# A reordered front of the expert layer in a two-layer diffusion backbone on one Trainium2 core

## The chip, the core and the metric

One NeuronCore of a Trainium2 chip runs the whole program. Its engines each have their own instruction stream: PE (TensorE, matrix products into the eight banks of PSUM), DVE (VectorE), ACT (ScalarE), POOL (GpSimd, which here issues the gathers) and SP (SyncE, which issues plain loads). Streams are ordered among each other by semaphores alone. The metric is the device time of the program in microseconds (us).

## What is computed

The reference is one inference step of a trunk of two layers over 640 tokens (128 context, 512 latent) of width 1024, in float32. Layer 0 mixes tokens by windowed attention beside a Mamba-2 scan, layer 1 by a bidirectional gated recurrence. Each layer then applies an output projection and a mixer of single-neuron experts (PEER), and this is the part that matters here:

```python
        out, new = even_mixer(h, P, j, ctx)        # or odd_mixer; ends in  mix @ w_out
        x = x + g1 * out
        h = rms_norm(x, P['norm_ffn'][l]) * (1 + sc2) + sh2
        x = x + g2 * peer(h, P, l)
...
def peer(h, P, l):
    q = (x @ P['p_w_q'][l]).reshape(m, PEER_HEADS, 2, PEER_DKEY)
    s = jnp.einsum('mhpd,hpnd->mhpn', q, P['p_sub_keys'][l])
    top_s, top_i = lax.top_k(s, PEER_TOPK)
    cand_s = top_s[:, :, 0, :, None] + top_s[:, :, 1, None, :]
    best_s, best_pos = lax.top_k(cand_s, PEER_TOPK)
    act = jax.nn.gelu(jnp.einsum('pd,phkd->phk', xb, u[eb])) * softmax(best_s)
    out = jnp.einsum('phk,phkd->pd', act, v[eb])
```

Every token picks 16 experts for each of 8 heads, so 128 rows of 4 KB from the table u and 128 from the table v.

## The kernel before

The tokens lie as 5 tiles of 128. `project_and_peer` runs once per layer. Its **front** is: the output projection of the five tiles, the update of x, the normalised input of the experts for tile 0, the router scores of tile 0, and the first top-k. Its **loop** is 40 steps g (tile t = g // 8, head i = g % 8); each step gathers 16 rows of u and 16 of v for every token (a gather is 512 KB and is one POOL instruction), takes 16 dot products with u on DVE, and adds 16 weighted rows of v on PE.

Nothing schedules this code: each engine runs its list in the order in which it is written, and waits where a `wait_ge` stands. The lists are:

- **PE.** In layer 0 first 40 transposes of the mixed rows (`rows(t, c)`, 8 per tile, L561, into banks 0 and 1, so each tile waits until ACT has copied the one before out at L494); layer 1 has these already. Then `project(t, b)`: tile t times half b of the output weights, 8 products into bank 6 + b (L533), with `score(0, n)` (a quarter of the router scores of tile 0, L553) and `turn(0)` (8 transposes of the normalised tile, L541) between them. `project(t, b)` for t >= 1 waits until DVE has read the same bank for tile t - 1 (`so.ev`). After all of them come the expert sums (L596).
- **DVE.** `projected(t)`: for both halves multiply the bank by the gate (L364) and add to x (L367). `normed(t)` (L373, L374). `topk(g)`: from L383 (first maximum) to L409 (the 16 expert numbers). `head(g)`: 16 dots (L429) and a tail of small operations to the weights at L445. The order is projected 0, normed 0, projected 1, topk 0, projected 2, topk 1, copy of the tile to PSUM (`h2p`, L457), topk 2, head 0 (with projected 3 after its eighth dot), topk 3, projected 4, head 1, and then topk(g + 2), head(g).
- **ACT.** Copies of transposes and scores out of PSUM (L494, L483, L488), the statistics of x (L476 to L478), and in the loop the diagonal weight matrices (L521).
- **POOL.** For each slot in turn the gather of u for step g (L344) and that of v for step g - 1 (L352), each into a ring of 8 buffers: a gather of u waits for the dot that reads its buffer (`s.ufree`), one of v for the sums that read it (`s.vfree`). Alone the first gather of v waits besides for all ten projections (`so.mm` at 10, a wait that ends at L533), since its ring lies over the output weights.
- **SP.** In layer 0 half 0 of the output weights (`load_out`, L1213), then in both layers the router weights of 6 MB and 2 MB (L298, L299), and behind them two modulation rows spread over all partitions (`bcp`, L301), which `normed(0)` reads. Half 1 of the output weights is loaded earlier, in `attention`.

Of the kernel before, what the change touches and what calls it, by code (L numbers as in the profile page):

```python
# [295 lines left out]
def router_weights(m, sp, l):  # L296

    sp.dma_start(m.wqA[:, :, :], m.wqk_rows[l][:, 0:12, :]).then_inc(m.sems.pw.h, 16)  # L298
    sp.dma_start(m.wqB[:, :, :], m.wqk_rows[l][:, 12:16, :]).then_inc(m.sems.pw.h, 16)  # L299
    for k in range(2):  # L300
        sp.dma_start(m.bcp[:, k, :], m.mod[l * 12 + 3 + k:l * 12 + 4 + k, :].to_broadcast([P, D])).then_inc(m.sems.pbc.h, 16)  # L301


def project_and_peer(nc, m, l, out):
# [8 lines left out]

    with nc.Block() as block:
        @block.sync
        def _(sp):
            if rows:
                load_out(m, sp, m.w_out, 0)
# [36 lines left out]
        def _(dve):  # L355
            ch = Link(dve, s.cv)

            def projected(t):
                for b in range(2):
# [4 lines left out]
                    nc.vector.tensor_tensor(m.oproj[:, :], ps[6 + b][:, :], m.gate[:, cond_of(t), b * 512:(b + 1) * 512], ALU.mult).then_inc(so.ev.h, 1)  # L364
# [54 lines left out]
            def head(g):  # L419
# [32 lines left out]
            projected(2)  # L452
            topk(1)
            for g in range(STEPS):
# [16 lines left out]
        def _(act):  # L471
# [8 lines left out]
            def turned(t):  # L480
                act.wait_ge(s.ptp.h, s.ptp.at(t + 1))
                for b in range(2):
                    q = nc.scalar.activation(m.phT[:, 4 * b:4 * b + 4, :], ps[(2 if t == 0 else 6) + b][:, :].rearrange("p (c t) -> p c t", c=4), ACT.Copy)  # L483
                q.then_inc(s.pht.h, 1)

            def scored(t, n):
                act.wait_ge(s.pqp.h, s.pqp.at(4 * t + n + 1))
                nc.scalar.activation(m.S[:, t % 2, n * 512:(n + 1) * 512], ps[n if t == 0 else 6 + n % 2][:, :], ACT.Copy).then_inc(s.pse.h, 1)  # L488

            if rows:  # L490
                for t in range(TILES):
                    act.wait_ge(so.tp.h, so.tp.at(t + 1))
                    for b in range(2):
                        q = nc.scalar.activation(m.mixT[:, t, 4 * b:4 * b + 4, :], ps[b][:, :].rearrange("p (c t) -> p c t", c=4), ACT.Copy)  # L494
                    q.then_inc(so.tpe.h, 1)
            statistics(0)
            turned(0)
            scored(0, 0)
            scored(0, 1)
# [1329 lines left out]
```

## Time and profile before

| | us |
|---|---|
| median of three runs | 4979.14 |
| lowest, highest of them | 4977.14, 4986.17 |
| the profiled execution, its own time | 4986.78 |
| span of the profiled execution, first to last instruction | 4984.9 |
| front of layer 0, from the first transpose to the first gather of v | 679.76 to 795.11 |
| front of layer 1, from the first projection to the first gather of v | 3195.12 to 3303.70 |

The profile gives for one execution each engine's busy time, what it waited for, and a timeline. The loops fill most of the span. PE is busy for 3952.8 us (79%), DVE for 3105.3 us (62%), POOL for 2672.2 us (54%), and 1508.39 MB pass through the 16 DMA engines, 1347.37 MB of them as gathers. A wait is put down to what ended it; an engine's idle time counts only where something later waits for that engine.

### The profile page before, as it was taken

The page shows a single profiled execution, that of the slowest core. Times are in us where ns is not written, and L with a number is a line of the kernel's source. Part 1 is how long each engine was busy: PE and PEld are TensorE (multiplying, and loading weights), DVE is VectorE, ACT ScalarE, POOL GpSimd, SP SyncE. Part 2 cuts the span into 40 slices and gives each one's busy share as a digit, 9 for nine tenths or more (in the row PEclk, how much of TensorE's full clock was granted, in tenths as well). Part 3 has the DMA queues.
Part 4 walks back from the last instruction along what each step waited for, and adds up shares of the span by engine and source line. Part 5 has one row for each costly group of instructions (what it writes and reads, how often), then busy time and mean ns, then how long its engine had stood idle before and what let it go on. Part 6 is the DMA issues. An engine that isn't in the chain of part 4 may idle for free. (4 is left out here: it accounts for less than half of the span.)

```text
span 4984.9 us, 41356 instructions
## 1 busy us (share of the span) xinstructions
PE 3952.8 (79%) x11732; PEld 1830.7 (37%) x11732; DVE 3105.3 (62%) x8304; ACT 1054.0 (21%) x2804; POOL 2672.2 (54%) x2872
## 2 busy tenths in 40 slices
PE   6596698887877877877788888587878879779777
PEld 2354563332322322322256665432323323223222
DVE  0124747777777677676425656377677777777774
ACT  1202231111111111111235454101111111111111
POOL 1100005777777777777532322047777777777775
PEclk8896799999999999999999999799999999999999
DMA  9910028999999999999911011169999999999998
GB/s 391 370 48 10 24 97 309 397 402 405 395 404 404 389 409 405 386 404 409 335 50 47 24 47 36 77 259 409 390 409 394 401 402 392 409 408 392 409 408 347
DMA packets 456205, 1508.39 MB, mean 303 GB/s; under 512 B 50838, under 2 KB 99894, under 8 KB 455228
## 3 DMA queue, kind: packets, MB, share of 16 engines
q0 software_dynamic: 371104, 1347.37, 68.5%
q1 hardware_dynamic: 80284, 141.82, 7.9%
q10 hardware_dynamic: 4608, 16.78, 0.8%
q8 instruction: 86, 1.41, 0.1%
q14 instruction: 123, 1.01, 0.1%
HBM read 1484.84 MB, written 20.94 MB: 302 GB/s over the span
## 5 line engine op out<-in xcount | busy, mean ns | idle before, releaser
L596 PE MATMUL psall<-work 128*128 128x512 f32 x5120 | 2445.6, 609 | 650.3 <-DMA work<-in_p_v,idx 586.5
L429 DVE CUSTOM_DVE_ANT_0 work<-work,psall 128x1024 f32<-128x1024 f32 x1280 | 1519.3, 1219 | 870.3 <-DMA work<-in_p_u,idx 869.7
L344 POOL DMA_INDIRECT work<-in_p_u,idx x1280 | 1214.5, 949 | 977.1 <-DVE idx L409 479.5
L596 PEld LDWEIGHTS psall<-work 128*128 128x128 f32 x5120 | 891.8, 190 | 2199.1 <-issue 1118.5
L352 POOL DMA_INDIRECT work<-in_p_v,idx x1280 | 1216.1, 950 | 498.2 <-issue 332.2
L521 ACT ACTIVATE work<-ident,work 128x128 f32<-128x128 f32 x1280 | 487.4, 399 | 1935.0 <-PE psall L596 1896.6
L1375 PE MATMUL psall<-work 128*128 128x512 f32 x640 | 284.1, 597 | 9.0 <-ACT work L1467 5.3
L553 PE MATMUL psall<-work 128*128 128x512 f32 x640 | 278.3, 592 | 0.0
L1348 POOL TENSOR_SCALAR work<-work 128x256 f32<-128x256 f32 x40 | 33.8, 844 | 381.2 <-ACT work L1459 381.2
L1570 DVE TENSOR_TENSOR work<-psall,work 128x128 f32<-128x128 f32 x560 | 116.7, 285 | 99.1 <-ACT work L1486 99.1
L553 PEld LDWEIGHTS psall<-work 128*128 128x128 f32 x640 | 121.6, 190 | 153.1 <-issue 153.1
L1375 PEld LDWEIGHTS psall<-work 128*128 128x128 f32 x640 | 119.5, 192 | 145.6 <-issue 145.6
L533 PE MATMUL psall<-work 128*128 128x512 f32 x320 | 150.5, 631 | 24.1 <-DVE work L364 21.7
L511 ACT ACTIVATE work<-work 128x16 f32<-128x16 f32 x80 | 17.3, 216 | 658.3 <-DVE work L435 658.3
L220 DVE TENSOR_TENSOR work<-psall,work 2x512 f32<-2x512 f32 x24 | 16.4, 684 | 197.3 <-PE psall L173 197.1
L157 POOL DMA_DIRECT2D mod_rows<-work x24 | 12.0, 506 | 199.4 <-DVE work L220 101.3
L173 PE MATMUL psall<-work 128*2 128x512 f32 x384 | 78.2, 691 | 48.0 <-DMA work<-in_w_ada 47.8
L1538 DVE TENSOR_TENSOR work<-psall,ident 128x128 f32<-128x128 f32 x40 | 11.7, 292 | 153.9 <-PE psall L1428 153.9
L429 DVE DVE_READ_ACCUMULATOR2_ANT work<- 128x1 f32 x1280 | 105.3, 82 | 0.0
L533 PEld LDWEIGHTS psall<-work 128*128 128x128 f32 x320 | 64.6, 204 | 107.2 <-issue 82.2
L1543 DVE COPY_PREDICATED work<-lmask,psall 128x128 f32<-128x128 uint8 x280 | 84.5, 302 | 29.6 <-DVE work L1543 1.4
L774 PE MATMUL psall<-work 128*128 128x512 f32 (+2 forms) x320 | 99.0, 470 | 0.0
(274 smaller groups left out, 3684.5 us busy)
## 6 DMA issues: line engine op xcount, KB each, us to landing
work<-in_w_ada SPq DMA_DIRECT2D x64, 768.0 KB, 12.3
work<-in_p_u,idx POOLq DMA_INDIRECT x1280, 8.2
work<-in_p_v,idx POOLq DMA_INDIRECT x1280, 8.3
work<-in_o_w_in SPq DMA_DIRECT2D x40, 512.0 KB, 7.0
work<-in_p_w_qT SPq DMA_DIRECT2D x32, 512.0 KB, 13.8
wqk_rows<-work ACTq DMA_DIRECT2D x32, 512.0 KB, 7.3
work<-wqk_rows SPq DMA_DIRECT2D x2, 6144.0 KB, 20.7
work<-mod_rows SPq DMA_DIRECT2D x16, 512.0 KB, 9.3
```

What stands on the lines that cost most here:

```text
L173: q = nc.tensor.matmul(m.ps[3 * (g % 2) + j][32 * j:32 * j + 2, :], m.condT[:, k, :], m.wa[:, n % WRING, j * 512:(j + 1) * 512], start=(k ...
L344: nc.gpsimd.indirect_dma_start(m.ur[:, b, :], None, u_flat, bass.IndirectOffsetOnAxis(ap=e, axis=0)).then_inc(s.ud[b].h, 16)
L352: nc.gpsimd.indirect_dma_start(m.vr[:, b, :], None, v_flat, bass.IndirectOffsetOnAxis(ap=e, axis=0)).then_inc(s.vd[b].h, 16)
L429: nc.vector.tensor_tensor_reduce(m.ur[:, b, :], m.ur[:, b, :], m.h2p[:, :], 1.0, 0.0, ALU.mult, ALU.add, m.d16[:, j:j + 1]).then_inc(s.ufr ...
L521: nc.scalar.activation(m.dgb[:, j % DIAGS, :], m.ident[:, :], ACT.Copy, scale=m.wt[:, t % 2, i * TOPK + j:i * TOPK + j + 1]).then_inc(s.dg ...
L533: q = nc.tensor.matmul(ps[6 + b][:, :], m.mixT[:, t, k, :], m.ew[:, b, k, :], start=(k == 0), stop=(k == KC - 1))
L553: q = nc.tensor.matmul(ps[n if t == 0 else 6 + n % 2][:, :], m.phT[:, k, :], w[:, :, k * P:(k + 1) * P], start=(k == 0), stop=(k == KC - 1))
L596: q = nc.tensor.matmul(o[:, k * 512:(k + 1) * 512], m.dgb[:, j % DIAGS, :], m.vr[:, b, k * 512:(k + 1) * 512], start=(i == 0 and j == 0), ...
L774: q = nc.tensor.matmul(m.ps[n % 8][:, 0:width], m.hT[:, k, c * P:(c + 1) * P], m.ew[:, p % 2, k, 0:width], start=(k == 0), stop=(k == KC - 1))
L1375: nc.tensor.matmul(ps[0][:, :], m.hT[:, k, t * P:(t + 1) * P], m.ow[:, b, k, 0:4, :].rearrange("p g n -> p (g n)"), start=(k == 0), stop=( ...
L1543: q = nc.vector.copy_predicated(m.So[:, t, :], m.lmask[:, l, :], ps[5 + r // 4][:, (r % 4) * P:(r % 4 + 1) * P])
L1570: q = nc.vector.tensor_tensor(out_v, in_v, ref, ALU.subtract)
```

## The change

It edits the front alone, in both layers, and one pair of buffers of attention.

1. The projections alternate between two pairs of banks: even tiles in 6 and 7, odd tiles in 0 and 1 (`bank(t)`). `project(t, b)` now waits for the read of tile t - 2.
2. The transposes of the mixed rows in layer 0 alternate between banks 4, 5 and 2, 3 and are spread over the front: tiles 0 and 1, two projections, tiles 2 and 3, and tile 4 behind `score(0, 0)`. `turn(0)` uses banks 4 and 5, the scores of tile 0 banks 2 and 3. ACT's copies follow (`mixed(t)`).
3. PE takes the projections of tile 3 ahead of `score(0, 1)`.
4. DVE runs topk 0, topk 1, then the copy to `h2p` (behind the copies out of those banks), projected 2 and head 0. Topk 2 and projected 4 come after head 0, and topk 3 stands after the eighth dot of head 1.
5. SP loads the `bcp` rows ahead of the router weights. Half 0 of the output weights of layer 0 is loaded in `attention`, whose buffers `pr` and `pT` move out of its place.
6. Two new waits: POOL's first gather of u in layer 0 waits for the last transposes of the mixed rows, and PE's first expert sum waits until DVE has read tile 3's projection (before: until ACT had copied two score banks).

```diff
 def router_weights(m, sp, l):
+    for k in range(2):
+        sp.dma_start(m.bcp[:, k, :], ...).then_inc(m.sems.pbc.h, 16)
     sp.dma_start(m.wqA[:, :, :], m.wqk_rows[l][:, 0:12, :]).then_inc(m.sems.pw.h, 16)
     sp.dma_start(m.wqB[:, :, :], m.wqk_rows[l][:, 12:16, :]).then_inc(m.sems.pw.h, 16)
-    for k in range(2):
-        sp.dma_start(m.bcp[:, k, :], ...).then_inc(m.sems.pbc.h, 16)
...
+    def bank(t):
+        return 6 if t % 2 == 0 else 0
...
-            if rows:
-                load_out(m, sp, m.w_out, 0)
...
                             pool.wait_ge(s.ix.h, s.ix.at(g + 1))
+                            if g == 0 and rows:
+                                pool.wait_ge(so.tp.h, so.tp.at(TILES))
...
                     if g == 0 and j == RING:
                         projected(3)
+                    if g == 1 and j == RING:
+                        topk(3)
...
             topk(0)
-            projected(2)
             topk(1)
+            dve.wait_ge(s.pht.h, s.pht.at(1))
+            if rows:
+                dve.wait_ge(so.tpe.h, so.tpe.at(TILES))
...
-                if g + 2 < STEPS:
+                if g == 0:
+                    projected(2)
+                elif g == 1:
+                    topk(2)
+                    projected(4)
+                elif g + 2 < STEPS:
                     topk(g + 2)
-                if g == 1:
-                    projected(4)
                 head(g)
...
             def project(t, b):
                 if t == 0:
                     pe.wait_ge(sw[b].h, sw[b].at(16))
-                else:
-                    pe.wait_ge(so.ev.h, so.ev.at(2 * t + b - 1))
+                if t >= 2:
+                    pe.wait_ge(so.ev.h, so.ev.at(2 * t + b - 3))
+                if rows and b == 0:
+                    pe.wait_ge(so.tpe.h, so.tpe.at(t + 1))
...
+            mix(0)
+            mix(1)
             project(0, 0)
             project(0, 1)
+            mix(2)
+            mix(3)
             project(1, 0)
             turn(0)
             project(1, 1)
             score(0, 0)
+            mix(4)
             project(2, 0)
             project(2, 1)
+            project(3, 0)
+            project(3, 1)
             score(0, 1)
-            for t in (3, 4):
-                project(t, 0)
-                project(t, 1)
+            project(4, 0)
+            project(4, 1)
             score(0, 2)
             score(0, 3)
...
-    q = Arena(st)
+    q = Arena(15360)
     m.pr = q.take(3, 512)
     m.pT = q.take(2, 512)
...
+            load_out(m, sp, m.e_w_out[0], 0)
             load_out(m, sp, m.e_w_out[0], 1)
```

PE's list in the front of layer 0, before. L561 are the transposes of the mixed rows, L533 projections (8 products each), L541 the turned tile, L553 scores, L596 expert sums:

```order
298 L561 MATMUL psall<-ident,work 128x128 x40
299 L533 MATMUL psall<-work 128x512 x24
300 L541 MATMUL psall<-ident,work 128x128 x8
301 L533 MATMUL psall<-work 128x512 x8
302 L553 MATMUL psall<-work 128x512 x8
303 L533 MATMUL psall<-work 128x512 x16
304 L553 MATMUL psall<-work 128x512 x8
305 L533 MATMUL psall<-work 128x512 x32
306 L553 MATMUL psall<-work 128x512 x16
307 L596 MATMUL psall<-work 128x512 x96
```

The same place now, where the lines are L584, L550, L560, L574 and L627 in that order:

```order
298 L584 MATMUL psall<-ident,work 128x128 x16
299 L550 MATMUL psall<-work 128x512 x16
300 L584 MATMUL psall<-ident,work 128x128 x16
301 L550 MATMUL psall<-work 128x512 x8
302 L560 MATMUL psall<-ident,work 128x128 x8
303 L550 MATMUL psall<-work 128x512 x8
304 L574 MATMUL psall<-work 128x512 x8
305 L584 MATMUL psall<-ident,work 128x128 x8
306 L550 MATMUL psall<-work 128x512 x32
307 L574 MATMUL psall<-work 128x512 x8
308 L550 MATMUL psall<-work 128x512 x16
309 L574 MATMUL psall<-work 128x512 x16
```

Sixteen transposes instead of 40 now stand ahead of the first projection, and four projections instead of two stand between the first and the second score; the counts are the same.

DVE's list around the second top-k of layer 0, before (L409 ends the second top-k, L457 is the copy to `h2p`, L383 begins the third top-k):

```order
393 L409 TENSOR_SCALAR idx<-work 128x16
394 L457 COPY psall<-work 128x1024
395 L383 MAX work<-work 128x8
396 L384 MAX_INDEX ti<-work 128x8
397 L385 MATCH_REPLACE work<-work 128x128
```

The same place now (L413 ends the second top-k, L465 is the copy, L368 and L371 are projected(2), L435 the first dot of head 0):

```order
389 L413 TENSOR_SCALAR idx<-work 128x16
390 L465 COPY psall<-work 128x1024
391 L368 TENSOR_TENSOR work<-psall,gate 128x512
392 L371 TENSOR_TENSOR x<-x,work 128x512
393 L368 TENSOR_TENSOR work<-psall,gate 128x512
394 L371 TENSOR_TENSOR x<-x,work 128x512
395 L427 TENSOR_TENSOR work<-work 128x16
396 L435 ISA work<-work,psall 128x1024
```

The third top-k has left the place between the copy and the first dot, and projected(2) has come from ahead of the second top-k to it.

## Rows read from the trace of the kernel before

**Rows 1.** the page's chain that ended last, share of the span by engine
```profile
DMA 9%; POOL 9%; DVE 8%; PE 5%; issue 4%; ACT 0%; SPq 0%; DVEq 0%; POOLq 0%
```

**Rows 2.** stretches: us; busy (count) of PE, PEld, DVE, ACT, POOL; clock; DMA; GB/s
```profile
679.70:695.40 15.70, 9.81 (x40) 7.84 (x40) 0.00 (x0) 5.42 (x10) 0.00 (x0) 0.50 0.96 382
744.00:795.00 51.00, 40.14 (x89) 17.43 (x88) 46.61 (x138) 2.31 (x7) 16.27 (x17) 0.90 0.50 175
860.00:2455.00 1595.00, 1280.97 (x2736) 476.51 (x2735) 1131.90 (x2911) 263.63 (x727) 1151.17 (x1215) 1.00 1.01 400
...
3236.00:3276.50 40.50, 40.37 (x95) 17.54 (x93) 30.19 (x112) 1.19 (x2) 7.62 (x8) 1.00 0.30 104
...
3370.00:4950.00 1580.00, 1266.04 (x2698) 471.50 (x2699) 1128.87 (x2903) 259.14 (x715) 1145.12 (x1205) 1.00 1.02 402
```

**Rows 3.** timeline, POOL, both fronts: start, us, operation, [idle before, releaser]
```profile
744.13 1.03 POOL L344 DMA_INDIRECT work<-in_p_u,idx  x1 [329.76 <-DVE idx L409]
...
752.94 0.94 POOL L344 DMA_INDIRECT work<-in_p_u,idx  x1 [0.31 <-issue]
770.46 0.94 POOL L344 DMA_INDIRECT work<-in_p_u,idx  x1 [16.58 <-DVE work L429]
...
795.11 0.93 POOL L352 DMA_INDIRECT work<-in_p_v,idx  x1 [11.22 <-PE psall L533]
...
859.35 0.94 POOL L344 DMA_INDIRECT work<-in_p_u,idx  x1 [5.37 <-DVE work L429]
...
3303.70 0.94 POOL L352 DMA_INDIRECT work<-in_p_v,idx  x1 [11.42 <-PE psall L533]
```

**Rows 4.** timeline, PE, front of layer 0
```profile
679.76 1.94 PE L561 MATMUL psall<-ident,work 128*128 128x128 f32 x8 [4.88 <-PEq L1200]
...
695.46 23.59 PE L533 MATMUL psall<-work 128*128 128x512 f32 x48 [1.18 <-ACT work L494]
718.88 1.04 PE L541 MATMUL psall<-ident,work 128*128 128x128 f32 x8
719.75 7.03 PE L533 MATMUL psall<-work 128*128 128x512 f32 x16
726.62 7.03 PE L553 MATMUL psall<-work 128*128 128x512 f32 x16
...
778.84 15.99 PE L533 MATMUL psall<-work 128*128 128x512 f32 x32 [10.86 <-DVE work L364]
```

**Rows 5.** timeline, DVE, layer 0, from the first top-k to the second head
```profile
734.32 0.30 DVE L383 MAX8 work<-work 128x8 f32<-128x128 f32 x1 [6.08 <-ACT work L488]
...
743.68 0.17 DVE L409 TENSOR_SCALAR idx<-work 128x16 uint32<-128x16 f32 x1
...
778.10 0.69 DVE L364 TENSOR_TENSOR work<-psall,gate 128x512 f32<-128x512 f32 x1
...
824.47 1.22 DVE L429 CUSTOM_DVE_ANT_0 work<-work,psall 128x1024 f32<-128x1024 f32 x1 [1.33 <-DMA work<-in_p_u,idx]
...
844.95 1.22 DVE L429 CUSTOM_DVE_ANT_0 work<-work,psall 128x1024 f32<-128x1024 f32 x1 [1.33 <-DMA work<-in_p_u,idx]
```

**Rows 6.** timeline, PE, front of layer 1
```profile
3224.29 1.97 PE L541 MATMUL psall<-ident,work 128*128 128x128 f32 x8 [6.15 <-DVE work L374]
3226.05 9.12 PE L533 MATMUL psall<-work 128*128 128x512 f32 x16
...
3287.24 16.19 PE L533 MATMUL psall<-work 128*128 128x512 f32 x32 [10.87 <-DVE work L364]
```

**Rows 7.** timeline, DVE, layer 1, the first normalised tile
```profile
3221.69 1.28 DVE L373 SCALAR_TENSOR_TENSOR work<-x,rs,work 128x1024 f32<-128x1024 f32 x1 [8.96 <-DMA work<-mod_rows]
```

**Rows 8.** DMA issues of 3190 to 3230: count, KB each, us to landing
```profile
work<-mod_rows SPq DMA_DIRECT2D x2, 512.0 KB, 24.4
```

**Rows 9.** timeline, ACT, layer 1, the last step of the statistics of tile 0
```profile
3214.27 0.20 ACT L478 ACTIVATE rs<-ss 128x1 f32<-128x1 f32 x1
```

**Rows 10.** DMA issues of 679 to 720, the front of layer 0
```profile
work<-in_e_w_out SPq DMA_DIRECT2D x1, 2048.0 KB, 9.2
```

More of the change, by code:

```diff
@@ L482, in turned @@
                 for b in range(2):
-                    q = nc.scalar.activation(m.phT[:, 4 * b:4 * b + 4, :], ps[(2 if t == 0 else 6) + b][:, :].rearrange("p (c t) -> p c t", c=4), ACT.Copy)
+                    q = nc.scalar.activation(m.phT[:, 4 * b:4 * b + 4, :], ps[(4 if t == 0 else 6) + b][:, :].rearrange("p (c t) -> p c t", c=4), ACT.Copy)
                 q.then_inc(s.pht.h, 1)
@@ L487, in scored, with mixed @@
                 act.wait_ge(s.pqp.h, s.pqp.at(4 * t + n + 1))
-                nc.scalar.activation(m.S[:, t % 2, n * 512:(n + 1) * 512], ps[n if t == 0 else 6 + n % 2][:, :], ACT.Copy).then_inc(s.pse.h, 1)
-            if rows:
-                for t in range(TILES):
+                nc.scalar.activation(m.S[:, t % 2, n * 512:(n + 1) * 512], ps[(2 if t == 0 else 6) + n % 2][:, :], ACT.Copy).then_inc(s.pse.h, 1)
+            def mixed(t):
+                if rows:
                     act.wait_ge(so.tp.h, so.tp.at(t + 1))
                     for b in range(2):
-                        q = nc.scalar.activation(m.mixT[:, t, 4 * b:4 * b + 4, :], ps[b][:, :].rearrange("p (c t) -> p c t", c=4), ACT.Copy)
+                        q = nc.scalar.activation(m.mixT[:, t, 4 * b:4 * b + 4, :], ps[4 - 2 * (t % 2) + b][:, :].rearrange("p (c t) -> p c t", c=4), ACT.Copy)
                     q.then_inc(so.tpe.h, 1)
+            for t in range(4):
+                mixed(t)
             statistics(0)
@@ L498, in _ @@
             scored(0, 0)
+            mixed(4)
             scored(0, 1)
@@ L537, in turn @@
                 pe.wait_ge(s.phr.h, s.phr.at(t + 1))
+                if t == 0 and rows:
+                    pe.wait_ge(so.tpe.h, so.tpe.at(3))
                 if t == 1:
@@ L540, in turn @@
                 for k in range(KC):
-                    q = nc.tensor.transpose(ps[(2 if t == 0 else 6) + k // 4][:, (k % 4) * P:(k % 4 + 1) * P], m.ph[:, k * P:(k + 1) * P], m.ident[:, :])
+                    q = nc.tensor.transpose(ps[(4 if t == 0 else 6) + k // 4][:, (k % 4) * P:(k % 4 + 1) * P], m.ph[:, k * P:(k + 1) * P], m.ident[:, :])
                 q.then_inc(s.ptp.h, 1)
@@ L548, in score, with mix @@
                     pe.wait_ge(s.pht.h, s.pht.at(t + 1))
-                if t > 0 and n >= 2:
+                if n >= 2:
                     pe.wait_ge(s.pse.h, s.pse.at(4 * t + n - 1))
+                if rows and t == 0 and n == 0:
+                    pe.wait_ge(so.tpe.h, so.tpe.at(4))
                 w = m.wqB[:, :, :] if n == 3 else m.wqA[:, 4 * n:4 * n + 4, :]
                 for k in range(KC):
-                    q = nc.tensor.matmul(ps[n if t == 0 else 6 + n % 2][:, :], m.phT[:, k, :], w[:, :, k * P:(k + 1) * P], start=(k == 0), stop=(k == KC - 1))
+                    q = nc.tensor.matmul(ps[(2 if t == 0 else 6) + n % 2][:, :], m.phT[:, k, :], w[:, :, k * P:(k + 1) * P], start=(k == 0), stop=(k == KC - 1))
                 q.then_inc(s.pqp.h, 1)
-            if rows:
-                for t in range(TILES):
-                    if t >= 1:
-                        pe.wait_ge(so.tpe.h, so.tpe.at(t))
+            def mix(t):
+                if rows:
+                    if t >= 2:
+                        pe.wait_ge(so.tpe.h, so.tpe.at(t - 1))
+                    if t == 4:
+                        pe.wait_ge(s.pht.h, s.pht.at(1))
                     for c in range(KC):
-                        q = nc.tensor.transpose(ps[c // 4][:, (c % 4) * P:(c % 4 + 1) * P], rows(t, c), m.ident[:, :])
+                        q = nc.tensor.transpose(ps[4 - 2 * (t % 2) + c // 4][:, (c % 4) * P:(c % 4 + 1) * P], rows(t, c), m.ident[:, :])
                     q.then_inc(so.tp.h, 1)
-                pe.wait_ge(so.tpe.h, so.tpe.at(TILES))
+            mix(0)
+            mix(1)
             project(0, 0)
             project(0, 1)
+            mix(2)
+            mix(3)
             project(1, 0)
@@ L585, in _ @@
                     score(t + 1, 2 * i - 7)
-                if i == 0 and t < 2:
-                    pe.wait_ge(s.pse.h, s.pse.at(2 * t + 2))
+                if g == 0:
+                    pe.wait_ge(so.ev.h, so.ev.at(2 * TILES - 2))
+                if i == 0 and t == 1:
+                    pe.wait_ge(s.pse.h, s.pse.at(4))
                 if i == 0 and t >= 2:
```

6 lines of the change are left out of this document (3 added, 3 removed).

## The prediction

> **What bounds the kernel now.** I read the chain of waits first: DMA and POOL hold 9% each and DVE 8% of the span, PE 5% [rows 1]. This is a machine in which gathers, dots and sums release each other in turn, and the chain alone does not say which of them sets the pace. The stretches do [rows 2]: each row gives a stretch's length, the engines' busy times in it, the granted clock of PE and the DMA share. In the loop of layer 0 (860 to 2455) and of layer 1 (3370 to 4950) the DMA share is 1.01 and 1.02 at 400 and 402 GB/s, while PE is busy for 1281 of 1595 us, DVE for 1132 and POOL for 1151. So the loop is bound by the bytes of the gathers, whose number is fixed. In the front (744 to 795) the DMA share is 0.50. Time lost there is lost for good, since the engines that lag can't move the remaining bytes faster later.
>
> Which front event opens the stream? POOL's own rows [rows 3]: eight gathers of u from 744.13, a stall of 16.58 us until the first dot frees a buffer at 770.46, nine more gathers, then a stall of 11.22 us that ends with a projection (L533). From the first gather of v at 795.11 on the stream is full. In layer 1 the same gather issues at 3303.70, after 11.42 us on the same wait. I call this gather the **gate**. It waits for the tenth projection, so PE's list up to there is the path of each front, and the time of the kernel is the time of the two gates plus constants, as long as the 17 gathers of u ahead of a gate are done before it in both versions.
>
> **PE's path, part by part.** One block of eight 128x512 products takes 6.87 us (719.75 to 726.62), eight transposes at the same clock 0.87 us (718.88 to 719.75) [rows 4]. The count of blocks ahead of the gate is the same before and after: ten projections, two scores, one turn. What changes is what lies between them.
>
> Layer 0, transposes: the 40 hold PE from 679.76 to 695.46, 15.70 us, at a granted clock of 0.50 [rows 2, 4], since each tile waits for ACT's copy out of the same banks. Afterwards tiles 0 and 1 go to different pairs of banks, without that wait: two times 1.95 = 3.9 us at the same low clock. Tiles 2, 3 and 4 come behind projections, where the clock is high: 3 x 0.87 = 2.6 us. Saved: 15.7 - 3.9 - 2.6 = 9.2 us. The first projection starts at the low clock before and after, so that loss cancels. If the clock rose sooner because PE no longer pauses, up to 2.9 us more would come (the first three blocks took 718.88 - 695.46 = 23.4 us, not 20.6) [rows 4]; I take 0, the nearest row being the 15.7 us of transposes at 0.50.
>
> The Trainium skill, "TensorE: Matmul & The Clock Gate", section "Part 4: PE-mode transpose", states that the clock does not rise to full rate for transposes and gives about 275 ns for one. The row behind the projections disagrees on the rate: those eight took 1.04 us together, the eight at 679.76 took 1.94 [rows 4]. By the page, tiles 2 to 4 would cost 1.94 each, 3.2 us more, and the forecast below would be 4937.9.
>
> Layer 0, the stall before tile 3: PE idles 10.86 us for DVE's L364, since projected(3) stands behind eight dots and both tiles share banks [rows 4, 5], and the next two blocks take 15.99 us where two take 6.87 + 7.03 = 13.90 [rows 4]: 2.1 us of lower clock. With two pairs of banks tile 3 needs tile 1's read, done long before, and tile 4 needs tile 2's. Is that one in time? Topk 0 starts when the first score is out, 15.7 - 3.9 - 1.7 = 10.1 us earlier than its 734.32 (tile 4's transposes come later), so at 724.2, and ends 9.5 us on at 733.8; topk 1 ends at 743.3; the copy takes 1.2 and the first half of projected(2) 0.7 us, done at 745.2. PE reaches project(4, 0) two blocks ahead of the end, near 759. So the stall goes, with 14 us to spare. Saved: 10.9 + 2.1 = 13.0.
>
> Layer 0 in sum 22.1 us: gate at 773.0 instead of 795.1.
>
> Layer 1 has no mixed transposes. PE idles 6.15 us for the normalised tile [rows 6], which DVE starts at 3221.69 after 8.96 us on the modulation rows [rows 7]; these landed 24.4 us after their issue, behind 8 MB of router weights [rows 8]. Issued first, they are 1 MB ahead of everything. Then the statistics end the wait, at 3214.5 [rows 9], and turn(0), 2.6 us of DVE later (3221.69 to 3224.29), follows the third projection (PE got there at 3224.3 - 6.15 = 3218.1) directly. Saved: 6.15, the turn at high clock 1.97 - 1.04 = 0.9, and the block after it 9.12 - 7.03 = 2.1 us [rows 4, 6]: 9.2. What is late next is the router weights, needed by the first score, now at 3235.0 - 9.1 = 3225.9. The last of the same four loads had landed by 3221.7 [rows 7], and no order of them moves more bytes, so 4 us are left. Then the stall of 10.87 us and 16.19 - 13.90 = 2.3 us of low clock behind it go as above [rows 6]. Layer 1 in sum 22.3 us: gate at 3281.4 on the old scale instead of 3303.7.
>
> **DVE's moved steps.** Moving topk 2 behind head 0 lets the first dot start at 733.8 + 9.5 + 1.2 + 2.8 (four operations of 0.69) = 747.3 instead of near 769 (its end released POOL at 770.46) [rows 3, 5]. Eight dots of at most 1.22, projected(3), eight more and the tail end near 772; topk 2 and projected(4) follow, and head 1 starts near 784, 11 us after the gate. All 17 gathers of u are out by 762, ahead of the gate, as assumed. In head 1 the eighth dot ran at gate + 29.4 and the last at gate + 49.8, both held back by their gathers [rows 5]. With topk 3 (9.5) after the eighth, dots 9 to 16 run from gate + 40.1 to at most + 49.9: they catch up. But the gather of u that needs dot 9 has its turn at about gate + 39 (31 issues at 1.26, POOL's pace while nothing stops it: seven in 8.81 us from 744.13 to 752.94 [rows 3]), so POOL may stall 2 us there, and the gathers of v queued behind it wait as well. I take 0 for this, because the next stall of before, 5.37 us at 859.35 (gate + 64) [rows 3], hangs on DVE's first dot of head 2, which does not move against the gate, and absorbs it; the DMA engines had a backlog through that one. The other end is the whole topk, 9.5 us per layer.
>
> **The rest.** POOL's new wait for tile 4's transposes: these end about 1 us after the first score, 9 us before the first expert numbers; it costs nothing, and if it came last everything on POOL would queue behind it. PE's new wait before the first sum is met at 760. Half 0 of the output weights took 9.2 us to land [rows 10]; issued at 679.7 it would hold up a projection that now starts at 683.7 by some 5 us, so its move into attention is needed, and there nothing else is in the way. Moving `pr` and `pT` costs nothing: same size, same operations. The ends of the layers, after the last gather, are untouched.
>
> **Sum.** 22.1 + 22.3 = 44.4 us. The profiled execution took 4986.8 (span 4984.9), so its like would take 4942.4. That execution was 7.6 us above the median of the three runs, 4979.1; against the median the forecast is 4934.7.
>
> **Rivals.** *Given back after the gate*: topk 3 inside head 1 starves the stream, and the stall of the full 9.5 us is not absorbed in either layer: 44.4 - 19 = 25.4 us, 4953.7. For it: the release that u needs really moves later by about that. Against it: the landing times, not DVE, set dots 9 to 16. 8%.
>
> *The front is longer than the path I see*, so that the stream ends where it did: the edit takes its stalls away, but something I count as absorbed (the pace of the loop) fixes the end, and the change doesn't bring what its order says: 4979. Against it: a DMA share of 1.01 over 1595 us. 4%.
>
> *Slower: the clock.* PE runs its front nearly without a pause. If the granted clock were held at its lower level of 1.2 GHz there, each of the 12 blocks per front would take 13.74 instead of 6.87 us: 82.4 more, less 22.2, twice: 5099. It decides at more than 22.2 / 6.87 = 3.2 blocks per layer at the low level. Against it: from 3236.0 to 3276.5 PE was busy for 40.37 of 40.50 us at a clock of 1.00 [rows 2]. 2%.
>
> *More*: the first blocks are warm, and the stall of 5.37 us after the gate, with its counterpart in layer 1, turns out to have cost DMA time and shrinks: 4924. 6%.
>
> **Numbers.** My case holds 80%: 4934.7. Its own uncertainty is the scatter of the runs (4977.1 to 4986.2, so 5 either way), up to 3.2 us for the transposes and 2.1 to 2.3 for a fall of the clock across the pair of tiles transposed between projections. The range reaches from 4920 (scatter below the case "more") to 4955 (the first rival). A difference of 0.2%, 10 us, is what a measurement of this kernel can tell from none. Faster by more: 0.94 (the case, "given back", "more"); within it 0.04; slower 0.02.
>
> **What would show it.** The first gather of v near 773 in layer 0, 93 us after the first transpose instead of 115.4; in layer 1 the gate 86.3 us after the first projection instead of 108.6. No idle time of PE over 1 us between the first transpose and the gate; a DMA share of 1.0 from the gate on. From gate to the end of each loop the same time as before within 3 us. The sum is wrong if PE waits for router weights in layer 1, if the stream shows a DMA share under 0.95 in the 66 us after a gate, or if transposes between projections take 1.9 us per tile.

## The result and the profile of the changed kernel

The changed kernel takes 4936.1 us (median of four runs, 4933.7 to 4942.2), beside 4979.7 for the kernel before in the same series: 43.6 us less, a ratio of 0.9912 with a 95% interval of 0.9900 to 0.9923. In a later series it took 4932.4 against 4979.6 (0.9910, 0.9893 to 0.9926). The forecast was 4934.7. Its profiled execution has a span of 4931.8 us, 53.1 less than that of before.

Start with layer 0's front. TensorE (PE), from the timeline of the changed kernel; the columns are start, duration, engine, line, operation, operands, count, and in brackets the idle time ahead with what ended it. L584 is the transposes of `mix`, L550 a projection, L560 `turn`, L574 a score block, answering [rows 4]:

```profile
675.66 3.65 PE L584 MATMUL psall<-ident,work 128*128 128x128 f32 x16 [4.88 <-PEq L1232]
679.10 14.14 PE L550 MATMUL psall<-work 128*128 128x512 f32 x32
693.07 1.91 PE L584 MATMUL psall<-ident,work 128*128 128x128 f32 x16
694.82 7.03 PE L550 MATMUL psall<-work 128*128 128x512 f32 x16
...
716.30 1.04 PE L584 MATMUL psall<-ident,work 128*128 128x128 f32 x8
717.17 27.63 PE L550 MATMUL psall<-work 128*128 128x512 f32 x64
744.64 7.03 PE L574 MATMUL psall<-work 128*128 128x512 f32 x16
751.50 13.90 PE L550 MATMUL psall<-work 128*128 128x512 f32 x32
```

Behind the first transpose no row carries a bracket: PE has no gap up to the last projection. The tenth projection ends at 765.2 and POOL (GpSimd) issues the first gather of v, the gate, at 765.67, 90.0 us after the first transpose; it was 115.4 [rows 3, 4]. POOL's stalls in the same stretch:

```profile
726.95 1.03 POOL L348 DMA_INDIRECT work<-in_p_u,idx  x1 [314.56 <-DVE idx L413]
741.79 0.94 POOL L348 DMA_INDIRECT work<-in_p_u,idx  x1 [5.07 <-DVE work L435]
754.29 0.94 POOL L348 DMA_INDIRECT work<-in_p_u,idx  x1 [2.63 <-DVE work L435]
765.67 0.94 POOL L356 DMA_INDIRECT work<-in_p_v,idx  x1 [10.45 <-PE psall L550]
806.68 0.93 POOL L348 DMA_INDIRECT work<-in_p_u,idx  x1 [2.23 <-DVE work L435]
829.65 0.94 POOL L348 DMA_INDIRECT work<-in_p_u,idx  x1 [3.42 <-DVE work L435]
```

The stall of 16.58 us for the first dot [rows 3] is now 5.07. The wait for a projection is still the last one ahead of the gate, so PE's list is still the path. Layer 1, PE and then POOL (answering [rows 6] and the last of [rows 3]):

```profile
3166.90 23.02 PE L550 MATMUL psall<-work 128*128 128x512 f32 x48 [1.17 <-PEq L1331]
3189.76 1.04 PE L560 MATMUL psall<-ident,work 128*128 128x128 f32 x8
3190.64 7.03 PE L550 MATMUL psall<-work 128*128 128x512 f32 x16
```

```profile
3252.87 0.94 POOL L356 DMA_INDIRECT work<-in_p_v,idx  x1 [9.58 <-PE psall L550]
```

The 6.15 us ahead of `turn(0)` are gone, and the gate is 86.0 us after the first projection instead of 108.6. The modulation rows land earlier (DMA issues of this stretch: size, us to landing; [rows 8] had 24.4):

```profile
work<-wqk_rows SPq DMA_DIRECT2D x1, 2048.0 KB, 24.5
work<-mod_rows SPq DMA_DIRECT2D x2, 512.0 KB, 5.2
```

Stretches of the changed kernel (length, then busy us of PE, PEld, DVE, ACT and POOL, granted clock of PE, DMA share, GB/s), answering [rows 2]:

```profile
675.60:679.10 3.50, 3.44 (x17) 3.47 (x17) 0.00 (x0) 1.09 (x2) 0.00 (x0) 0.50 0.66 206
679.10:693.00 13.90, 13.90 (x33) 6.18 (x33) 1.38 (x2) 1.09 (x2) 0.00 (x0) 0.98 1.06 446
693.00:765.00 72.00, 72.00 (x193) 33.80 (x192) 52.40 (x139) 8.55 (x20) 16.30 (x17) 1.00 0.43 159
765.70:860.00 94.30, 74.81 (x160) 27.77 (x158) 69.24 (x190) 14.27 (x39) 67.59 (x72) 1.00 1.00 392
860.00:2455.00 1595.00, 1272.98 (x2724) 475.29 (x2725) 1118.27 (x2875) 268.15 (x738) 1132.41 (x1193) 1.00 1.00 396
...
3166.90:3190.00 23.10, 23.10 (x51) 10.17 (x52) 5.32 (x7) 1.65 (x4) 0.00 (x0) 0.90 0.96 399
3252.90:3370.00 117.10, 92.45 (x196) 33.87 (x194) 92.44 (x251) 18.62 (x52) 82.64 (x87) 1.00 1.00 393
```

The DMA share is 1.00 from the gate on. The stretch from 860 to 2455 holds fewer gathers than before (1193 POOL instructions against 1215), but only because the last gather of v is issued at 2428.4 here and at 2455.4 before. Shifted by the 29.5 us that the gate moved, the loop is what it was (400 GB/s, [rows 2]):

```profile
830.50:2425.50 1595.00, 1278.11 (x2729) 475.00 (x2728) 1131.45 (x2911) 263.23 (x726) 1149.93 (x1214) 1.00 1.01 400
```

The clock tells something new. In layer 0 PE starts at 0.50 of full speed (1.2 of 2.4 GHz) and is at 0.98 from the first projection on, where before it stayed at 0.50 for the 15.7 us of the transposes. In layer 1 the first 23.1 us are at 0.90; the same three blocks take 23.02 us in both kernels.

**Where the 53.1 us of the spans come from.** The execution splits at four marks: the first transpose, gate 0, layer 1's first projection, gate 1.

| part (us) | before | after | difference |
|---|---|---|---|
| start to first transpose | 679.8 | 675.7 | -4.1 |
| to gate 0 | 115.4 | 90.0 | -25.3 |
| to layer 1's first projection | 2400.0 | 2401.2 | +1.2 |
| to gate 1 | 108.6 | 86.0 | -22.6 |
| to the end | 1681.2 | 1678.9 | -2.3 |

The fronts give 47.9. The 4.1 ahead of them have arisen before attention begins (its first product starts at 597.4 instead of 601.5), in code that does the same in both kernels; in the eleven other profiles below the first transpose falls anywhere from 672.2 to 680.7. That is where much of the scatter of whole times sits, so I judge the experiments by the marks first and by the medians second.

### The profile page after: what moved, and what is told of

It is laid out like the page before. It is cut to its first block and busy times, and to the rows that moved or that the text cites. A ratio compares the mean times of both kernels' runs of the same rounds, so it can differ in the third digit from the quotient of the medians.

```text
span 4931.8 us, 41363 instructions
## 1 busy us (share of the span) xinstructions
PE 3925.3 (80%) x11732; PEld 1816.5 (37%) x11732; DVE 3104.1 (63%) x8304; ACT 1053.6 (21%) x2804; POOL 2675.2 (54%) x2872
## 5 line engine op out<-in xcount | busy, mean ns | idle before, releaser
L627 PE MATMUL psall<-work 128*128 128x512 f32 x5120 | 2440.4, 607 | 655.8 <-DMA work<-in_p_v,idx 595.1
L435 DVE CUSTOM_DVE_ANT_0 work<-work,psall 128x1024 f32<-128x1024 f32 x1280 | 1518.6, 1219 | 850.4 <-DMA work<-in_p_u,idx 850.2
L627 PEld LDWEIGHTS psall<-work 128*128 128x128 f32 x5120 | 889.7, 189 | 2201.5 <-issue 1102.9
L574 PE MATMUL psall<-work 128*128 128x512 f32 x640 | 278.2, 592 | 0.0
L574 PEld LDWEIGHTS psall<-work 128*128 128x128 f32 x640 | 121.6, 190 | 153.1 <-issue 153.1
L1407 PEld LDWEIGHTS psall<-work 128*128 128x128 f32 x640 | 119.2, 191 | 145.0 <-issue 145.0
L550 PE MATMUL psall<-work 128*128 128x512 f32 x320 | 141.3, 600 | 1.2 <-PEq L1331 1.2
L435 DVE DVE_READ_ACCUMULATOR2_ANT work<- 128x1 f32 x1280 | 105.6, 82 | 0.0
L499 ACT ACTIVATE work<-psall 128x512 f32<-128x512 f32 x40 | 23.6, 596 | 319.7 <-PE psall L574 319.7
```

The lines of the kernel that those rows point to most:

```text
L435: nc.vector.tensor_tensor_reduce(m.ur[:, b, :], m.ur[:, b, :], m.h2p[:, :], 1.0, 0.0, ALU.mult, ALU.add, m.d16[:, j:j + 1]).then_inc(s.ufr ...
L550: q = nc.tensor.matmul(ps[bank(t) + b][:, :], m.mixT[:, t, k, :], m.ew[:, b, k, :], start=(k == 0), stop=(k == KC - 1))
L574: q = nc.tensor.matmul(ps[(2 if t == 0 else 6) + n % 2][:, :], m.phT[:, k, :], w[:, :, k * P:(k + 1) * P], start=(k == 0), stop=(k == KC - 1))
L627: q = nc.tensor.matmul(o[:, k * 512:(k + 1) * 512], m.dgb[:, j % DIAGS, :], m.vr[:, b, k * 512:(k + 1) * 512], start=(i == 0 and j == 0), ...
L1407: nc.tensor.matmul(ps[0][:, :], m.hT[:, k, t * P:(t + 1) * P], m.ow[:, b, k, 0:4, :].rearrange("p g n -> p (g n)"), start=(k == 0), stop=( ...
```

## The experiments

All start from the changed kernel ("after"). Distances are in us: gate 0 from the first transpose, gate 1 from layer 1's first projection, and what follows each.

| kernel | gate 0 | on to layer 1 | gate 1 | on to the end | median | ratio to before (95%) |
|---|---|---|---|---|---|---|
| before | 115.4 | 2400.0 | 108.6 | 1681.2 | 4979 to 4980 | |
| after, first series | 90.0 | 2401.2 | 86.0 | 1678.9 | 4936.1 | 0.9912 (0.9900-0.9923) |
| k after again | 90.1 | 2401.3 | 86.0 | 1680.4 | 4932.4 | 0.9910 (0.9893-0.9926) |
| a score(0,1) last, p4 first | 83.4 | 2401.5 | 79.1 | 1680.4 | 4921.8 | 0.9883 (0.9868-0.9898) |
| h score(0,1) last | 83.4 | 2401.5 | 79.1 | 1679.9 | 4924.3 | 0.9887 (0.9872-0.9902) |
| b modulation rows last | 93.4 | 2401.4 | 93.4 | 1678.8 | 4945.9 | 0.9930 (0.9917-0.9944) |
| c one pair of banks | 99.0 | 2399.4 | 95.7 | 1680.7 | 4954.0 | 0.9950 (0.9937-0.9964) |
| d top-k's early | 101.5 | 2400.1 | 97.4 | 1677.2 | 4953.1 | 0.9948 (0.9934-0.9961) |
| e transposes first | 90.3 | 2401.2 | 86.0 | 1677.4 | 4936.8 | 0.9911 (0.9898-0.9925) |
| i the same in one pair | 97.4 | 2401.0 | 86.0 | 1678.6 | 4940.6 | 0.9923 (0.9906-0.9939) |
| f half 0 of ew late | 98.1 | 2396.7 | 86.0 | 1679.9 | 4940.9 | 0.9923 (0.9909-0.9937) |
| g topk(3) ahead of head 1 | 90.2 | 2398.0 | 86.0 | 1679.3 | 4934.2 | 0.9908 (0.9893-0.9923) |
| j gate in halves, first half | 72.4 | 2408.7 | 69.2 | 1687.7 | 4922.4 | 0.9887 (0.9870-0.9903) |

In j the gate opens in two halves, and its row gives the first. In the other twelve rows gate 0 moves over 32 us and gate 1 over 30; what follows them stays within 2396.7 to 2401.5 and 1677.2 to 1681.2. That is the main proposition of the prediction, shown over twelve executions; j shows where it ends.

**a. Open the gate one block earlier.**

```diff
-            score(0, 1)
             project(4, 0)
             project(4, 1)
+            score(0, 1)
...
-                    topk(2)
                     projected(4)
+                    topk(2)
```

> After with the second score block of tile 0, score(0,1), moved behind both blocks of project(4), and on DVE the rest of tile 4's projection (projected(4)) ahead of the third top-k. It asks whether the first gather of v (the gate) still sets the end one for one. Theory 1 (the gate does): the gate opens one block of 6.87 us earlier in each layer, at 83.1 us after the first transpose in layer 0 (after: 90.0) and at 79.1 us after the first projection in layer 1 (after: 86.0); DVE's first 8 dots of head 1 stand idle 9.6 us in all for gathers of u that are issued behind the gate, so they move with it, and POOL's stalls stay at gate + 41 and gate + 64; 2 x 6.87 = 13.7 us less than after, 4922 us. Theory 2 (DVE's chain behind the gate is the bound): head 1 starts at the same time as in after, POOL's two stalls behind the gate grow by 6.9 us together, and the time stays at 4936 us.

POOL's first gathers of v, layer 0 and layer 1:

```profile
760.00 0.93 POOL L356 DMA_INDIRECT work<-in_p_v,idx  x1 [3.61 <-PE psall L550]
3240.59 0.94 POOL L356 DMA_INDIRECT work<-in_p_v,idx  x1 [2.72 <-PE psall L550]
```

83.4 and 79.1 us, and the time fell by 14.3 against the first series of after (10.7 against the second): theory 1. But not in every detail. POOL's stalls behind the gate did not keep their places: there is one of 3.80 us at gate + 23, none at gate + 41, and 1.36 at gate + 64. The DMA share over the 66 us behind the gate is 0.98, as in after, so the stream passed over them.

**h. The same without moving DVE's (VectorE's) third top-k.** It keeps only the first part of a's edit, the one in PE's list.

> As the version with score(0,1) behind project(4), but DVE's order is that of after (third top-k, then projected(4)). The top-k waits for the second scores' copy (766.5 instead of 763.6), so head 1 starts 2.9 us later while the gate is 6.87 us earlier. Theory 1: head 1's first 8 dots have 9.6 us of idle time to give: still 12 to 13.7 us less than after, 4923 us. Theory 2 (DVE's chain is the bound): 2.9 us a layer more than after, 4942 us.

Theory 1 again: the same gates, 4924.3 us, which can't be told from a. DVE's later start is absorbed.

**b. Modulation rows behind the router weights.**

```diff
-    for k in range(2):
-        sp.dma_start(m.bcp[:, k, :], ...)
     sp.dma_start(m.wqA[:, :, :], ...)
     sp.dma_start(m.wqB[:, :, :], ...)
+    for k in range(2):
+        sp.dma_start(m.bcp[:, k, :], ...)
```

> After with the two loads of modulation rows behind the router weights again, all else kept. Theory 1: layer 0 stays as it is (gate 90.0 us after the first transpose); in layer 1 the rows land some 24.4 us after their issue instead of 5.2, DVE's product waits for them, TensorE waits 6.2 us ahead of the transposes of turn(0), which then and the block behind run slower (0.9 + 2.1 us): the gate is at 95.2 us after the first projection (after: 86.0), 9.2 us more in all, 4945 us. Theory 2 (the second pair of banks takes up the wait, the clock does nothing): 0 to 6 us more. Theory 3 (the load order was worth nothing): 4936 us.

`turn(0)` of layer 0, then `turn(0)` and the block behind it in layer 1:

```profile
710.06 1.09 PE L560 MATMUL psall<-ident,work 128*128 128x128 f32 x8 [3.09 <-DVE work L378]
...
3204.36 1.97 PE L560 MATMUL psall<-ident,work 128*128 128x128 f32 x8 [5.81 <-DVE work L378]
3206.12 7.59 PE L550 MATMUL psall<-work 128*128 128x512 f32 x16
```

Layer 1 loses 7.4 us: 5.8 of wait, 0.9 in the transposes, 0.6 in the block (2.1 were expected; the clock came back sooner). Layer 0 was expected to stay and lost 3.4, with a wait of 3.09 of the same kind. Before, TensorE came so late to `turn(0)` there that the rows were hidden, though they landed 28.5 us after their issue (the output weights were ahead of them too); in b they land after 24.6 us, but 9.6 us of transposes are gone, and the wait shows. So the load order protects layer 0's gain too: 10.8 us in both gates together, 9.8 in the median against the first series.

**c. One pair of banks.**

```diff
-        return 6 if t % 2 == 0 else 0
+        return 6
...
-                if t >= 2:
-                    pe.wait_ge(so.ev.h, so.ev.at(2 * t + b - 3))
+                if t >= 1:
+                    pe.wait_ge(so.ev.h, so.ev.at(2 * t + b - 1))
```

> After with all projections in one pair of banks (6 and 7), as before; the order on all engines, the transposes and the loads are those of after. Theory 1 (most of the stall before tile 3 went through DVE's order, since projected(2) now runs at 737.4 and not behind two top-k's): project(3,0) wants to start at 730.9 and waits for the first half of projected(2), 738.1, so 7.2 us in each layer, and TensorE's clock or its fall adds 0 to 2.1 us; project(1) and project(2) wait for nothing; the gate is 7.2 to 9.3 us later in each layer, 14 to 19 us in all, 4952 us. Theory 2 (the banks themselves carry the whole term): 10.9 + 2.1 us in each layer, 26 us, 4962 us. Theory 3 (order alone was enough): 4936 us.

`project(3, 0)` in layer 0 and in layer 1:

```profile
737.73 15.50 PE L550 MATMUL psall<-work 128*128 128x512 f32 x32 [7.04 <-DVE work L368]
3232.75 15.56 PE L550 MATMUL psall<-work 128*128 128x512 f32 x32 [7.89 <-DVE work L368]
```

Theory 1, at its upper end: waits of 7.0 and 7.9 us (DVE's read of tile 2), and 15.5 us for two blocks that take 13.9 without the pause: 9.0 and 9.7 us in the gates (expected were 7.2 to 9.3 each), 17.9 in the median.

**d. DVE's old order.**

```diff
                 if g == 0:
                     projected(2)
+                    topk(2)
                 elif g == 1:
-                    topk(2)
+                    topk(3)
                     projected(4)
...
-                    if g == 1 and j == RING:
-                        topk(3)
```

> After with DVE's order of before among the pieces: topk(2) ahead of the dots of head 0, topk(3) ahead of those of head 1; TensorE's order, banks and loads are those of after. Theory 1: topk(2) must wait for the second score block (751.5, copied by 752.3) and ends at 761.5, so head 0's first dot falls from 740.3 to 761.6, the u ring frees late, POOL reaches the first gather of v at 776 instead of 765.7 (+10.3 in each layer), then a stall of about 3.8 us replaces the two of 2.2 and 3.4: +8.5 us a layer, 17 us in all, 4953 us. Theory 2 (TensorE's list alone sets the gate, DVE's order is worth nothing): 4936 us. Theory 3 (all of it is lost): 4980 us.

POOL's ninth gather of u and its first of v, layer 0 (L433 is the dots' line here):

```profile
767.84 0.94 POOL L348 DMA_INDIRECT work<-in_p_u,idx  x1 [26.65 <-DVE work L433]
780.33 0.93 POOL L348 DMA_INDIRECT work<-in_p_u,idx  x1 [2.63 <-DVE work L433]
781.56 0.94 POOL L356 DMA_INDIRECT work<-in_p_v,idx  x1 [0.30 <-issue]
```

Theory 1: the first gather of v waits for nothing but its turn behind 17 gathers of u, which the dots hold up. PE's projections are as early as in after, and it doesn't help: +11.4 us at each gate (10.3 expected), +17.0 in the median against the first series of after, +20.7 against the second (17 expected). What theory 1 had wrong is the part behind the gate: no single stall replaced the two of after, there are again two, of 3.42 and 2.60 us, and from the gates on the profile is only 1.1 and 1.7 us shorter. "The gate waits for PE's tenth projection" is true only while the dots come first.

**e. Transposes of four tiles first.** `mix(2)` and `mix(3)` stand ahead of `project(0, 0)`.

> After with the transposes of tiles 0 to 3 all ahead of the first projection (after: two tiles, then the projection of tile 0, then two tiles). Layer 0 only. Theory 1 (gaps keep the clock low): TensorE waits for ScalarE's copies (1.09 us each, two a tile) ahead of tiles 2 and 3, the first projection starts at about 8.2 us after the first transpose instead of 3.4, and its first block runs at the low clock again, as before (2.9 us more): gate at 95.8 us after the first transpose (after: 90.0), +5.8 us, 4942 us. Theory 2 (the copies cost, the clock has risen by itself): +2.9 us, gate at 92.9, 4939 us. Theory 3 (only the work counts): 0. In layer 1 nothing changes (gate 86.0).

```profile
680.14 5.92 PE L584 MATMUL psall<-ident,work 128*128 128x128 f32 x32 [4.88 <-PEq L1232]
685.89 20.77 PE L550 MATMUL psall<-work 128*128 128x512 f32 x48
```

Only the work counted: gate at 90.3. My expectation misread ScalarE's copies: the row shows 1.09 us for two, not for one, so with two pairs of banks the transposes never wait. The clock, stretch by stretch:

```profile
680.10:683.60 3.50, 3.46 (x17) 3.49 (x18) 0.00 (x0) 1.09 (x2) 0.00 (x0) 0.50 0.64 198
683.60:686.00 2.40, 2.40 (x18) 2.17 (x17) 0.00 (x0) 2.07 (x4) 0.00 (x0) 0.85 1.22 454
686.00:700.00 14.00, 14.00 (x34) 6.17 (x33) 1.55 (x3) 1.18 (x3) 0.00 (x0) 1.00 0.98 425
```

It rose while PE was doing transposes alone: 0.50 in their first 3.5 us, 0.85 in the next 2.4. The Trainium skill, "TensorE: Matmul & The Clock Gate", section "Part 4: PE-mode transpose", says that it does not rise for them; the measurement decides, for these f32 transposes of a kernel whose PE was busy until 4.9 us before.

**i. The same in one pair of banks.** `mix` and `mixed` use banks 4 and 5 only, so each tile waits for the copy of the one before.

> As the version with the transposes of tiles 0 to 3 all ahead of the first projection, but in one pair of banks, so that TensorE waits about 1.18 us for ScalarE's copies behind each tile, as before. In that version TensorE had no gap, the granted clock rose from 0.50 about 3.4 us after the first transpose, and the gate stood at 90.3 us. Theory 1 (the short gaps keep the clock at 1.2 GHz): each tile takes 1.96 + 1.18 = 3.14 us, the first projection starts 12.6 us after the first transpose, its first block runs at the low clock (2.5 to 2.9 us more), gate at 99.7 to 100.2 us in layer 0. Theory 2 (the clock rises some 3.4 us after work begins, gaps or not): from the second tile on 0.96 + 1.18 us a tile, the first projection at about 9.5 us, no slow block: gate at 94.1. Layer 1: 86.0 in both.

```profile
675.32 1.94 PE L584 MATMUL psall<-ident,work 128*128 128x128 f32 x8 [4.88 <-PEq L1232]
678.44 1.97 PE L584 MATMUL psall<-ident,work 128*128 128x128 f32 x8 [1.18 <-ACT work L505]
...
684.73 1.97 PE L584 MATMUL psall<-ident,work 128*128 128x128 f32 x8 [1.18 <-ACT work L505]
686.49 22.42 PE L550 MATMUL psall<-work 128*128 128x512 f32 x48
```

```profile
675.00:690.00 15.00, 11.15 (x37) 7.96 (x38) 0.02 (x1) 4.34 (x8) 0.00 (x0) 0.51 0.97 382
```

With pauses of 1.18 us the clock stays at 0.51, and all four tiles take 1.94 to 1.97 us: theory 1 in its mechanism. Its size was 2.3 to 2.8 us too large: the first projection does not wait for the last copy and starts at 11.2, and the first three blocks lose 1.65 us to the clock (22.42 against 20.77), not 2.5 to 2.9. The pauses cost 7.1 us at the gate against e, half of it waiting (3 x 1.18 = 3.5) and half the clock, 1.9 in the transposes and 1.65 in the blocks. In the median only 3.9 us of it appear; between these two kernels that is as far as medians resolve.

**f. Half 0 of the output weights late.** The load stands at the head of the expert layer again, ahead of the modulation rows.

> After with the first half of e_w_out loaded where before loads it, at the start of the expert layer, ahead of the modulation rows and router weights. Layer 0 only. Theory 1: the load lands 9.2 us after its issue at about the first transpose, while the first projection wants to start 3.4 us after it: TensorE waits 5.6 us, and stays or falls to the low clock, 0 to 2.9 us more: gate at 95.6 to 98.5 us after the first transpose (after: 90.0), +7 us, 4943 us. Theory 2 (hidden under the transposes): 0. The 2 MB ahead of the modulation rows cost nothing, since those have slack in layer 0.

```profile
683.99 16.59 PE L552 MATMUL psall<-work 128*128 128x512 f32 x32 [5.39 <-DMA work<-in_e_w_out]
```

Theory 1: 5.4 us of wait and 2.5 of clock, gate at 98.1. The median rose by 4.8 only (8.5 against the second series), and in this profile the way from gate 0 to layer 1 is 4.5 us shorter than in after. 4.2 of these lie in the loop: the last gather of v comes 1658.6 us behind the gate, against 1662.8 in after, 1660.6 in k and 1660.2 in before. I read that as scatter of the loop: c, d and g, which load the weights as after does, have 1658.9, 1659.1 and 1658.6. They carry edits of their own, so it is not shown, but a way this short does not need f's edit.

**g. topk(3) ahead of head 1.** The test of "given back after the gate".

> After with topk(3) ahead of the dots of head 1 instead of in their middle. Theory 1: head 1's first dot falls from 776.1 to 785.7; the u ring makes POOL wait 2.6 us at the ninth gather of u of head 1 (gate + 19) and about 2.6 us at gate + 61, in place of 2.2 at gate + 41 and 3.4 at gate + 64: within 1 us a layer, 4936 us (4934 to 4939). Theory 2 (the gain is given back behind the gate when this top-k stands ahead): +9.2 us a layer, 4954 us.

```profile
790.90 0.94 POOL L348 DMA_INDIRECT work<-in_p_u,idx  x1 [2.56 <-DVE work L433]
...
833.47 0.94 POOL L348 DMA_INDIRECT work<-in_p_u,idx  x1 [2.61 <-DVE work L433]
```

Both stalls have the size that theory 1 gave them and lie within 3 us of its places (gate + 21 and + 64, expected + 19 and + 61), and the time is 4934.2: the middle of head 1 was not a needed place for this top-k.

**j. The gate in halves.** The first half of `ew` lies under the first four buffers of v. `project(4, 0)` moves ahead of `project(3, 1)`, POOL takes four gathers of v in between:

```diff
...
+            for n in range(13):
+                up(n)
+            for n in range(4):
+                down(n)
+                up(13 + n)
+            for n in range(17, 21):
+                up(n)
...
```

Score blocks, projected(3), projected(4), topk(2) and topk(3) move as well, as the expectation lists.

> Built on what the other runs showed: the gate sets the end, so it is opened by halves. ew's first half lies under the v ring's slots 0 to 3 and its second under slots 4 to 7. TensorE runs project(4,0) ahead of project(3,1), so that the first half is free 13.7 us ahead of the second; POOL issues the first four gathers of v between those of u of head 0 and goes on with u up to the 21st; score(0,1) stands behind the projections, score(0,2) and (0,3) between the first sums (or the v ring would wait for them), projected(3) behind head 0's dots, topk(2) behind head 1's fourth dot, topk(3) with projected(4) behind its twelfth. Theory 1: POOL has no stall from 66 us after the first transpose on, the first gather of v is issued at 72.4 us (version with one gate: 83.4), the fifth at 87.2 (there 93.3): 6 to 7 us less in each layer than that version's 4922 us, 4909 us (4906 to 4914). Theory 2 (the u ring or DVE takes it up: head 0's last dots, pushed back by gathers of v, or a stall behind topk(2)): 4922 us. Theory 3 (the early gathers of v delay those of u so far that sums and top-k fall behind): over 4930 us.

POOL's first and fifth gather of v, then the longest later stalls:

```profile
748.41 0.94 POOL L359 DMA_INDIRECT work<-in_p_v,idx  x1 [0.30 <-issue]
...
763.34 0.94 POOL L359 DMA_INDIRECT work<-in_p_v,idx  x1 [0.30 <-issue]
...
786.99 0.94 POOL L347 DMA_INDIRECT work<-in_p_u,idx  x1 [3.71 <-DVE work L452]
...
802.89 0.93 POOL L359 DMA_INDIRECT work<-in_p_v,idx  x1 [4.09 <-PE psall L643]
```

PE's first sums:

```profile
770.82 9.48 PE L643 MATMUL psall<-work 128*128 128x512 f32 x16 [4.58 <-DVE work L384]
```

The stream opened as computed, with the first and the fifth gather 72.4 and 87.3 us after the first transpose (a's first: 83.4). Then the sums could not keep up: PE waited 4.58 us for `projected(3)` (L384), which I had moved, the 16 matrix instructions of the sums behind that pause took 9.48 us where the next 16 take 7.03 (granted clock 0.87 from 763 to 790, 1.00 from 790 on), and POOL then waited 4.09 us for PE at L643, a wait that a does not have. The stall of 3.71 us for DVE behind topk(2), which theory 2 named, is there too, but a has one like it (3.80). By the marks layer 0 ends 3.8 us and layer 1 2.6 us earlier than in a, although their first gathers of v are issued 11.0 and 9.9 us earlier; the medians, 4922.4 and 4921.8, show no gain. So theory 1, 6 to 7 us a layer, fell, and the time is that of theory 2. How much of the loss comes from the moved `projected(3)` and how much from opening the gate this early stays open, since no run changes one without the other. In this order, opening the gate earlier no longer pays one for one.

**k. After again.**

> The changed kernel itself once more, beside the two versions of this series, as the point of comparison: 4936 us (4932 to 4940), ratio to the kernel before 0.991; gate at 90.0 and 86.0 us as in its first profile. If its median falls outside this range, differences of some microseconds between series are not to be read.

As expected. Medians of one kernel differ by 3.7 us between series, so single differences under some 5 us are left to the marks.

## Why the prediction was right, point by point

- **The gate is the path of each front, and time lost there is lost for good.** Right, and shown by the table above: a moved it the good way, b, c, d the bad way, and the rest of the layer stayed the same.
- **Layer 0's transposes, 9.2 us.** They now take 3.44 ahead of the first projection, 1.75 for tiles 2 and 3 and 0.87 for tile 4, 6.1 in sum instead of 15.7: 9.6.
- **Warmer first blocks, taken at 0 with 2.9 as the bound.** This is the term that was mis-sized. The first three blocks took 20.84 us, start to start, instead of 23.42: 2.6 saved. I had let the row of 15.7 us at 0.50 [rows 2] stand for "transposes run cold"; e and i show that the pauses of 1.18 us between tiles kept it so, and the change removes just those.
- **The stall before tile 3, 13.0.** What is left of 25.3 is 13.1. But it needed two things at once: c (banks alone taken away) costs 9.0, d (DVE's order alone) 11.4. As a stall of PE it hangs on the banks: c has most of it back, d none of it. But in d the gate opens late all the same, because the prediction's condition, that the 17 gathers of u are done ahead of the gate, no longer holds. The two prices add up to more than the term, so neither may be read as its share.
- **Layer 1, 22.3 in sum.** Measured 22.6. Router weights came in time, though they landed 24.5 us after their issue instead of 22.7: no idle ahead of the score block. The clock's part in the block behind `turn(0)` was 2.1 us in the old trace and 0.6 in b; the size of such a fall is not a constant of the wait.
- **The load order costs and gives nothing in layer 0.** Not stated so, but the sum had no term for it there. b shows that 3.4 us of layer 0's saving rest on it.
- **Stall near gate + 39, absorbed.** 2.23 us at gate + 41, and the next at gate + 64 fell from 5.37 to 3.42. The sum of both hardly changed, and from gate to layer 1 it is 1.2 us more than before.
- **The sum.** Marks: 47.9 instead of 44.4, the difference being the warm blocks (2.6), and under a microsecond of remainders. The medians differ by 43.6 and 47.2 in the two series. That the first falls within 1 us of the forecast is partly luck: the forecast of the fronts was 3.5 us short.
- **The rivals.** "Given back" fell with g, which provokes it and loses nothing. "Front longer than the path" fell with the marks. "Slower by the clock" fell with the clock: 0.98 to 1.00 from layer 0's first projection on, and in layer 1 0.90 for three blocks, as before, then no slower block. Of "more", the first half came true.
- **Transposes behind projections.** The eight at 716.30 took 1.04 us; the 1.94 a tile of the low clock, which the prediction set beside the rule of the Trainium skill ("TensorE: Matmul & The Clock Gate", section "Part 4: PE-mode transpose") did not come.

## What to carry over

Find the one event behind which the bound resource is full, and measure every edit by its distance to a fixed mark ahead of it; whole times scatter by several microseconds here from parts that no edit touches. Before crediting a stall to one cause, take each of the pieces that remove it away alone: here buffers, engine order and load order each held the gate by 3 to 11 us a layer. When a wait is removed, ask which load had been hidden under it, and watch, as in j, whether the dots and sums behind the event still keep up when it is pulled further forward.

## What the runs showed of the hardware

- Short pauses can hold TensorE's clock at its lower level: 1.18 us behind each 1.97 us of transposes kept it at 0.50 to 0.51 for 11 to 16 us (before, i), while without pauses it was 0.50 for the first 3.5 us of transposes and 0.85 to 0.98 in the stretch behind (e, after).
- A fall of the clock behind a pause has no fixed price: behind 5.8 to 7.9 us of idle time, two blocks lost 1.6 us (c) and `turn(0)` with its block 1.5 (b), where the trace of before had 2.1 to 3.0 behind 6.15 and 10.87 us.
- The order on one queue decides when a load lands: 1 MB of modulation rows lands in 4.6 and 5.2 us when first (after), in 24.3 to 24.6 behind 8 MB of router weights (b, and layer 1 of before), whose last part itself takes 24.5 and 25.0 us behind the rows instead of 22.5 to 22.8.
